# A two-layer decoder trunk on eight cores: weights copied in bf16 within DRAM by casting transfers, and read back by SyncE's queue

## The reference

```python
def reference(x, ...):
    for i in range(DEPTH):                       # 2
        h = rmsnorm(x, norm_mix_g[i])
        if i % N_MIXERS == 0:
            x = x + mlstm_mixer(h, ...)          # q, k: 4 heads x 128; v: 4 heads x 256
        else:
            x = x + gla_mixer(h, ...)
        h = rmsnorm(x, norm_ffn_g[i])
        x = x + sq_relu_mlp(h, ffn_w1[i], ffn_w2[i])
    return rmsnorm(x, final_norm_g)

def sq_relu_mlp(xn, w1, w2):                     # w1: 1024 x 4096, w2: 4096 x 1024
    hid = jnp.square(jax.nn.relu(xn @ w1))
    return hid @ w2
```

## Time and profile before

| | |
|---|---|
| median of 3 runs | 1383.59 us (1382.86 to 1412.55) |
| profiled execution, slowest core | 1391.73 us |
| its span (core 1) | 1390.7 us |
| spans of the eight cores | 1367.9 to 1390.7 us |
| TensorE, VectorE, ScalarE, GpSimd busy | 96%, 69%, 54%, 17% of the span |
| mean clock of core 0, of core 1 | 0.998, 0.991 |
| HBM read, written (per core) | 176.46 MB, 8.39 MB |
| q0, casting transfers from GpSimd | 91.92 MB, 49.3% of 16 engines |
| q1, SyncE's transfers | 25.20 MB, 8.4% of 16 engines |

### The profile page before, as it was taken

One profiled execution on the slowest core, in us unless ns is written; L12 is line 12 of the kernel. 1 busy time (PEld: TensorE's weight loads), 2 busy tenths in 40 slices (PEclk: granted clock), 3 DMA queues, 4 the chain that ended last, 5 costly groups with the idle time before them and its releaser, 6 DMA issues.

```text
span 1390.7 us, 23130 instructions; the slowest of 8 cores (1367.9 to 1390.7 us)
## 1 busy us (share of the span) xinstructions
PE 1332.4 (96%) x6813; PEld 626.5 (45%) x6813; DVE 955.3 (69%) x2088; ACT 753.7 (54%) x1606; POOL 233.6 (17%) x263
## 2 busy tenths in 40 slices
PE   5999999899999999999999999999999999998997
PEld 2555554443444444444444545444344444443445
DVE  2398384957468967567658867677665888876836
ACT  2496665636158267185248765664541953842565
POOL 6020110211111111112013001040111111111114
PEclk9999999999999999999999999999999999999998
DMA  9955211368587496758774101034747857778853
GB/s 165 228 106 104 44 32 23 51 72 101 73 96 92 61 106 81 90 63 108 111 145 100 39 16 31 16 45 59 91 61 93 105 75 84 93 130 129 101 73 122
DMA packets 202011, 118.86 MB, mean 85 GB/s; under 512 B 53872, under 2 KB 187168, under 8 KB 201888
## 3 DMA queue, kind: packets, MB, share of 16 engines
q0 software_dynamic: 143392, 91.92, 49.3%
q1 hardware_dynamic: 57968, 25.20, 8.4%
q10 hardware_dynamic: 528, 0.26, 0.1%
HBM read 176.46 MB, written 8.39 MB: 133 GB/s over the span
## 4 chain that ended last, share of the span: by engine, by line
PE 80%; DMA 10%; DVE 5%; issue 3%; ACT 1%; POOL 1%; DVEq 0%; SPq 0%; ACTq 0%; POOLq 0%
PE ps L260 80%; DMA wraw_68<-w 3%; DMA wraw_72<-w 2%; DMA wqk<-m_win 2%; DMA wraw_69<-w 1%; DMA wraw_73<-w 1%; DVE xT L270 1%; DMA wraw_71<-w 1%; DVE Cbf L1145 1%; DVE R_110 L274 0%; DVE NB L1018 0%; DVE rt L279 0%; DVE hn L274 0%; DMA ktok_102<-kx_150 0%; POOL wqk L217 0%
## 5 line engine op out<-in xcount | busy, mean ns | idle before, releaser
L266 ACT ACTIVATE ps<-ps 128x512 f32<-128x512 f32 x184 | 106.6, 585 | 192.2 <-PE ps L260 159.9
L270 DVE TENSOR_TENSOR xT<-ps,xT 128x512 f32<-128x512 f32 (+2 forms) x224 | 142.6, 649 | 91.7 <-PE ps L260 91.4
L266 ACT ACTIVATE rt<-ps 128x512 f32<-128x512 f32 x156 | 91.6, 592 | 93.0 <-PE ps L260 91.6
L266 ACT ACTIVATE sq<-xT 128x512 f32<-128x512 f32 x128 | 78.6, 626 | 31.5 <-DVE sd L270 13.1
L274 DVE SCALAR_TENSOR_TENSOR R_110<-R_110,egs,ps 128x256 f32<-128x256 f32 x112 | 53.0, 474 | 14.4 <-PE ps L260 13.4
L266 ACT ACTIVATE junk<-ps 128x256 bf16<-128x256 f32 x128 | 49.1, 384 | 25.2 <-DVE ps L270 14.2
L270 POOL TENSOR_TENSOR sd<-sd,sq 128x512 f32<-128x512 f32 x40 | 51.2, 1279 | 38.9 <-ACT sq L266 31.5
L270 POOL TENSOR_TENSOR sd<-sq 128x512 f32<-128x512 f32 x8 | 10.3, 1293 | 276.2 <-ACT sq L266 266.9
L217 POOL DMA_DIRECT2D wraw_68<-w x23 | 20.2, 878 | 203.4 <-PE ps L260 77.6
L1145 DVE TENSOR_SCALAR Cbf<-R_110,egs 128x256 bf16<-128x256 f32 x120 | 46.9, 425 | 0.9
L279 DVE CUSTOM_DVE_ANT_0 rt<-ps,rt 128x512 f32<-128x512 f32 x43 | 29.4, 687 | 21.3 <-PE ps L260 21.1
(11 more groups left out here) (842 smaller groups left out, 3609.5 us busy)
## 6 DMA issues: line engine op xcount, KB each, us to landing
wraw_68<-w POOLq DMA_DIRECT2D x23, 512.0 KB, 7.5
wraw_73<-w POOLq DMA_DIRECT2D x22, 512.0 KB, 7.8
wraw_69<-w POOLq DMA_DIRECT2D x21, 512.0 KB, 8.1
wraw_72<-w POOLq DMA_DIRECT2D x21, 512.0 KB, 7.7
wraw_71<-w POOLq DMA_DIRECT2D x20, 512.0 KB, 7.7
wraw_70<-w POOLq DMA_DIRECT2D x19, 512.0 KB, 7.8
outT<-xT SPq DMA_DIRECT2D x12, 512.0 KB, 5.2
xT<-xT POOLq DMA_DIRECT2D x6, 512.0 KB, 33.3
```

The costliest lines, as they stand in the source:

```text
L266: t.op("act", lambda e: e.activation(out=out, in_=in_, func=func, **kw), r=r, w=w, ns=190 + 0.84 * n + (80 if acc is not None else 0))
L270: t.op(eng, lambda e: e.tensor_tensor(out=out, in0=in0, in1=in1, op=op), r=r, w=w, ns=170 + 1.03 * n if eng == "dve" else 200 + 2.2 * n)
```

## The change

Two arrays are added in DRAM, `w16` (a bf16 copy of each slab, 4 KB to a partition, in the order in which a slab lies in SBUF) and `in16` (a bf16 copy of the second mixer's q, k, v and r weights). Casting transfers on GpSimd's queue fill them, DRAM to DRAM:

- 20 slabs of layer 0 (the sixteen of w2, and 2 to 5 of w1) in chunks 4 to 13 of the first mixer, two per chunk, behind `gate(c)`;
- the eight row blocks of `in16` (128 x 3072) at steps 3, 5, ... 17 of the first MLP, and slabs 20 to 31 of layer 1 at steps 19, 21, ... 41;
- slabs 0 to 19 of layer 1 in chunks 4 to 13 of the second mixer, behind `gate(c)`.

`load` asks whether the slab has been copied: if so SyncE's queue loads 512 KB of bf16, if not GpSimd's queue casts as before. In layer 0 that makes 40 loads by SyncE and 24 by GpSimd, in layer 1 64 by SyncE. `load_in16` replaces `load_cols` for the second mixer, on SyncE's queue. No compute instruction is added or removed.

```diff
+    def convert(out, in_, key, gate=()):
+        i = cv[0] % 4
+        cv[0] += 1
+        t.dma("pool", [(out, in_)], 1048576, r=gate, w=[key, ("cv", i)], sem="cv%d" % i)
+    def convert_in(k):
+        convert(in16_d[:, k:k + 1, :], g_win_d.rearrange("(k p) n -> p k n", p=128)[:, k:k + 1, 0:3072], ("in16", k))
+    def load_in16(dst, nm, c0, ks):
+        t.dma("sp", [(dst[:, ks[0]:ks[-1] + 1, :], in16_d[:, ks[0]:ks[-1] + 1, c0:c0 + 1024])], len(ks) * 262144,
+              r=[("in16", k) for k in ks], w=[(nm, hf, k) for hf in range(2) for k in ks])
...
+        def to16(s, i, gate=()):
+            s.conv.add(i)
+            convert(w16_d[s.L, i].rearrange("p (k n) -> p k n", n=256), s.src(i), ("w16", s.L, i), gate)
...
         def load(s, gate=()):
             sl = s.slabs[s.nload]
             s.nload += 1
             i = sl["slot"]
-            t.dma("pool", [(wraw[i][:].rearrange("p k a n -> p k (a n)"), sl["src"])], 1048576, r=gate,
-                  w=[("wr", i), ("w3", i)], sem="slab%d" % i)
+            w = [("wr", i), ("w3", i)]
+            if sl["id"] in s.conv:
+                t.dma("sp", [(wraw[i][:].rearrange("p k a n -> p (k a n)"), w16_d[s.L, sl["id"]])], 524288,
+                      r=list(gate) + [("w16", s.L, sl["id"])], w=w, sem="slab16_%d" % i)
+            else:
+                t.dma("pool", [(wraw[i][:].rearrange("p k a n -> p k (a n)"), s.src(sl["id"]))], 1048576, r=gate, w=w,
+                      sem="slab%d" % i)
...
+    CONV = (list(range(16, 32)) + [2, 3, 4, 5], list(range(20)))
...
+        for n, i in enumerate(CONV[layer]):
+            c = n // 2 + 4
+            add(c, (-1,), [lambda i=i, c=c: f.to16(i, mx.gate(c))])
...
+    for k in range(KC):
+        hooks.setdefault(3 + 2 * k, []).append(lambda k=k: convert_in(k))
+    for n, i in enumerate(range(20, 32)):
+        hooks.setdefault(19 + 2 * n, []).append(lambda i=i: ffn[1].to16(i))
```

More of the change, by code:

```diff
@@ L254, in build @@
     out_d = dram("outT", [D, T], kind="ExternalOutput")
+    w16_d = nc.dram_tensor("w16", [2, 32, 128, 2048], BF16, kind="Internal").ap()
+    in16_d = nc.dram_tensor("in16", [128, KC, 3072], BF16, kind="Internal").ap()
     es = ExitStack()
@@ L597, in __init__ @@
         def __init__(s, layer, slot_of, steps):
-            s.L, s.steps, s.slabs = layer, steps, []
-            w1v = w1_d[layer].rearrange("(k p) n -> p k n", p=128)
-            w2v = w2_d[layer].rearrange("(k p) n -> p k n", p=128)
+            s.L, s.steps, s.slabs, s.conv = layer, steps, [], set()
             for st in steps:
@@ L603, in __init__ @@
                 if st["kind"] == "up":
-                    srcs = [w1v[:, :, st["P"] * 256:(st["P"] + 1) * 256]]
+                    ids = [st["P"]]
                 else:
-                    srcs = [w2v[:, (st["P0"] + 4 * h) * 2:(st["P0"] + 4 * h) * 2 + 8, st["jp"] * 256:(st["jp"] + 1) * 256]
-                            for h in range(st["np"] // 4)]
-                for v in srcs:
+                    ids = [16 + (st["P0"] + 4 * h) + st["jp"] for h in range(st["np"] // 4)]
+                for v in ids:
                     n = len(s.slabs)
                     st["slabs"].append(n)
-                    s.slabs.append(dict(src=v, slot=slot_of(n), wino=st["wino"]))
+                    s.slabs.append(dict(id=v, slot=slot_of(n), wino=st["wino"]))
             last = {}
@@ L616, in __init__, with src @@
             s.nload, s.nsum = 0, 0
+        def src(s, i):
+            q, jp = divmod(i - 16, 4)
+            if i < 16:
+                return w1_d[s.L].rearrange("(k p) n -> p k n", p=128)[:, :, i * 256:(i + 1) * 256]
+            return w2_d[s.L].rearrange("(k p) n -> p k n", p=128)[:, q * 8:q * 8 + 8, jp * 256:(jp + 1) * 256]
+        def to16(s, i, gate=()):
+            s.conv.add(i)
+            convert(w16_d[s.L, i].rearrange("p (k n) -> p k n", n=256), s.src(i), ("w16", s.L, i), gate)
         def load(s, gate=()):
@@ L1434, in build @@
     st1 = stats_pe(1)
-    hooks[44] = xn_slots(1, 0, m1.gcol) + [lambda: load_cols(wqk, "wqk", g_win_d, 0, 4, range(4)), st1[0]]
-    hooks[45] = [st1[1], lambda: load_cols(wqk, "wqk", g_win_d, 0, 4, range(4, KC)), lambda: m1.zl_F(0),
+    hooks[44] = xn_slots(1, 0, m1.gcol) + [lambda: load_in16(wqk, "wqk", 0, range(4)), st1[0]]
+    hooks[45] = [st1[1], lambda: load_in16(wqk, "wqk", 0, range(4, KC)), lambda: m1.zl_F(0),
                  lambda: m1.z_F(0, 0)]
     hooks[46] = xn_slots(1, 1, m1.gcol)
-    hooks[47] = [lambda: load_cols(wv, "wv", g_win_d, 1024, 3, range(6))]
+    hooks[47] = [lambda: load_in16(wv, "wv", 1024, range(6))]
     F0.run(2, len(F0.steps), hooks)
-    load_cols(wv, "wv", g_win_d, 1024, 2, range(6, KC))
-    load_cols(wo, "wo", g_win_d, 2048, 4)
+    load_in16(wv, "wv", 1024, range(6, KC))
+    for ks in (range(4), range(4, KC)):
+        load_in16(wo, "wo", 2048, ks)
     ring["tmps"] = range(4)
```

1 line of the change is left out of this document (added).

## The result

The changed kernel took 1427.6 us at the median of four runs (1420.7 to 1431.1), the kernel before 1384.5 us beside it: a ratio of 1.031 (1.025 to 1.036). It is slower by 3.1%; the forecast was 1372 us. The profiled execution took 1420.7 us.

What follows compares the result with a forecast made beforehand. TensorE, busy 96%, was taken to lose time only to waits for slabs and the lower clock behind them. First MLP -4.5, second MLP -13, mixers +5 us gave about 12 us off 1383.59: 1372 us, range 1357 to 1398.

Steps and rivals of the forecast that it cites:

- What bounds the kernel: Whole kernel, core 1: TensorE busy 96%; only its idle time and lower clock can be won, 23.8 us in the slabs' stages.
- The slab load: bf16 slab loads on SyncE's queue: 2.4 us of engines instead of 4.2, 5 us to landing instead of 7.5.
- The second MLP: All 64 slab loads become SyncE's, no converting transfer there: 13 of 14.7 us won on core 1.
- The first MLP: 40 of 64 loads move to SyncE, copies added: 4.5 of 9.1 us won; bounds 9 won and 5 lost.
- a load behind a row block lands 6 us later: First MLP, casting queue: delay taken for a remaining casting load that comes behind a row block of the mixer's weights.
- The copy's price: Each DRAM-to-DRAM casting copy of a slab takes 4.2 us of engines, 6.6 us as the upper end.
- The mixers: Twenty copies added to each mixer cost 2.5 us per mixer, bounds 0 and 15, through late sums on GpSimd.
- 5 to 10 us late costs TensorE nothing: Mixers: ktok transposes are issued some 20 us ahead and hn needed a group later, so such delays are free.
- The sum: Core 1: 1390.7 - 4.5 - 13 + 5 = 1378.2 us; 12 us off the median of 1383.59 gives about 1372.
- A (given back): Copies in first MLP (-5) and mixers (5 each) cost the second MLP's gain: about 1385 us; chance 0.25 together with D.
- B: Copies clog the mixers at GpSimd's queue, chunks 12 and 13: 1406 us at 7.5 us a copy, 1426 at 8; chance 0.14.
- The signs named at its end: Would show it wrong: copies landing 12 us or more late, late GpSimd sums, TensorE waits in mixers, first MLP idle over 7.3 us.

## Why the prediction was wrong

**What bounds the kernel** held: waits for slabs, and the clock behind them. With slabs that land in 3.4 to 4.3 us they are nearly gone from the second MLP: from 1000 to 1340 us every core has at most 1.6 us idle, at a clock of 1.00.

**The slab load** was taken at 2.4 us of engines and 5 us to landing. Measured: 29.0% of 340 us is 98.6 us for 33.30 MB, so 1.55 us per 512 KB, stores among them; 3.4 to 4.3 us to landing. Between the bounds of 1.2 and 2.4, and faster than the value taken.

**The second MLP**, 13 us of 14.7 on core 1: its loss fell from 28.9 to 12.9 us there (end included). Right; at the mean of the cores it fell by 9.2 us, since core 1 was the worst one before. That a move between queues gives nothing by itself was right for this stage only: in the first MLP the move of the loads to SyncE is what let the copies run ahead.

**The first MLP** is the term that failed: 4.5 us won at the forecast, 5 lost at the bound, 24.1 lost at the mean. Its bytes were not too low: 45.6% and 17.0% of 432 us are 270 us of engine time, the sum had 297. The step that failed is "a load behind a row block lands 6 us later". It priced one row block in front of a load, as if the list of steps (3, 5, ... 17) were a timetable. It is an order of issue only: neither the eight row blocks nor the eleven slab copies had a gate, and the change itself had emptied GpSimd's queue of most of the slot-waiting loads that would have spaced them. What held them was a fifth copy's wait for the first (18.45 us at 442.89) or a casting load that waited for its slot in front of them (81.66 us at 387.18). The runs showed, in the step's place, loads that landed 21.22 and 36.54 us after their issue beside three or four row blocks. Four row blocks are 4 x 6.3 = 25 us of all engines; with that price for each of a few loads the bound would have lain far beyond 5 us. Spacing the copies by steps gave back 11 us, leaving the slab loads in GpSimd's queue 13. The other 11 to 13 us are not bunching. Bytes cost as well (38.6 us lost with every slab cast and the row blocks apart, 0.7 us for each spaced copy), but how the rest divides isn't settled.

A price for several casting transfers at once was on the page of the kernel before. At the start GpSimd issues them back to back, and those of 512 KB, which land in 7.5 to 8.1 us as slab loads, landed in 33 to 43 (core 1, timeline, then issues with KB and us):

```profile
15.31 2.94 POOL L217 DMA_DIRECT2D wo<-m_win  x4
```

```profile
xT<-xT POOLq DMA_DIRECT2D x6, 512.0 KB, 33.3
wo<-m_win POOLq DMA_DIRECT2D x4, 512.0 KB, 43.4
```

**The copy's price**, 4.2 us with 6.6 as the upper end: 4.15. Right.

**The mixers**, 2.5 us each: +9.1 and +3.7. The upper bound of 15 held at the mean only; the first mixer's loss rose by 19.7 us on core 2 and by 17.3 on core 4. The mechanism named (the gate holds up GpSimd, the sums come late) is one that the runs show, but at the sums of an earlier row block, about 200 us, and not only at those from 244 us on that the prediction looked at. The trace before has these sums too (core 1):

```profile
199.75 1.27 POOL L270 TENSOR_TENSOR sd<-sq 128x512 f32<-128x512 f32 x1 [39.34 <-ACT sq L266]
```

**"5 to 10 us late costs TensorE nothing"** failed for `ktok`. Beside x it was not issued some 20 us ahead: on core 2 of the changed kernel it was issued at 115.63 us and needed at 124.07, and TensorE waited 3.5 us for it at the mean of the cores. For `hn` the sentence overlooked the next writer of the one buffer, VectorE, which did wait (4.9 us); by the runs with two buffers that cost nothing measurable.

**The sum** ends on a step that does not follow: it finds 12.5 us for the profiled execution, says that the median's slowest core has less to win, and takes 12 off all the same. Beside a miss of 55.6 us this is small.

**The rivals.** A (given back) had the right place, the first MLP, with a loss five times too small. B had the right sign by luck: a copy took 4.15 us and not 6.6 or more, the mixers added 9.1 and 3.7 us and not 17 or more each, and most of the loss came in the first MLP. The range ended at 1398 because neither let more than one stall come from the first MLP.

**The signs named at its end** worked: landings of 12 us and more, late sums, waits of TensorE for `ktok`, more than 7.3 us idle in the first MLP all came, and the cores moved apart.

## What to carry to other kernels

A transfer that is placed at a step without a gate is only placed in a queue: ask what keeps the queue from running ahead, and price as many at once as its limit allows. A gate on a transfer holds everything behind it on that engine, so put it where the engine has nothing due; a stage whose own loads are always due has no quiet stretch. Look also for the wait that a run makes while it takes another away: the sums on VectorE ended ScalarE's wait and began TensorE's. Here the part that lies in the second mixer alone, with or without eight copies clear of the sums in the first, is faster than the kernel before by 0.4 to 0.5%.

## What the runs showed of the hardware

Cores come in pairs. In every execution of the changed kernel one of cores 0 and 1, of 2 and 3, of 4 and 5, of 6 and 7 is faster by 20 to 32 us (1389.2 and 1417.0, 1406.4 and 1381.1, 1419.6 and 1390.4, 1416.5 and 1388.2 in the profiled one), and which one changes from run to run; with only the second mixer's copies the two differ by 7 to 10 us in the profiled execution (1374.1 and 1364.2, 1359.4 and 1367.0). Before the change the two of a pair differ by 4.7 to 22.8 us. In the profiled execution of the changed kernel the row blocks landed later on the slower core of each pair, 25.8 to 34.2 us at the median against 18.5 to 25.7; whether that is cause or consequence is not shown. (The Trainium skill, HBM Reference, Specifications (TRN2), says that the two cores of a pair share one memory domain.) No run took one core of a pair out, so the cause is not shown.

A stall costs again in the clock: on core 4 of the changed kernel TensorE idled 8.9 and 9.3 us in 420 to 460 us, and the granted clock was 0.75 and 0.84 in these two stretches, a mixture of the levels 1.2 and 2.4 GHz. Over its first MLP 33.5 us idle came with 15.4 us lost to the clock.
